# Last attention's rope scores as two fp32r products over 128 rows, another order of ScalarE's copies and exps, two-product gate projections, a 352-wide input projection

## The reference

```python
# block 1: the forget gate is a projection of 16 columns of w_in
log_f = log_sigmoid(f_logit + b_forget); cum = cumsum(log_f)
...
# layer A: u = rms_norm(x) @ w_in; 8 of its columns are the gates
gates = gates + b_if
i_pre, log_f = gates[..., :4], log_sigmoid(gates[..., 4:])
...
# layer C
u = rms_norm(x, norm_g) @ w_in
cq, ckv, kpe, z = split(u, [384, 384 + 256, 384 + 256 + 64])
q = (rms_norm(cq, q_norm_g) @ w_uq).reshape(B, S, 8, 192)
kv = (rms_norm(ckv, kv_norm_g) @ w_ukv).reshape(B, S, 8, 128 + 128)
k = concatenate([k_nope, broadcast(kpe)])            # 128 + 64 columns a head
q = rms_norm(q, qn_g); k = rms_norm(k, kn_g)
q, k = [nope, rope(last 64 columns, cos, sin)]
s = einsum('bhqd,bhkd->bhqk', q, k) * 192 ** -0.5     # blocks of the causal mask: 128 x 128
o = softmax(s) @ v * silu(z);  x + o @ w_out
```

## Time and profile before

| | |
|---|---|
| median of the runs | 1853.67 us |
| lowest, highest | 1852.9, 1855.1 us |
| profiled execution, its time | 1853.72 us |
| its span in the profile | 1851.6 us |
| PE busy | 1729.0 us, 93% |
| DVE busy | 1157.1 us, 62% |
| ACT busy | 987.3 us, 53% |
| POOL busy | 230.9 us, 12% |

### The profile page before, as it was taken

One profiled execution on the slowest core, in us unless ns is written; L12 is line 12 of the kernel. 1 busy time (PEld: TensorE's weight loads), 2 busy tenths in 40 slices (PEclk: granted clock), 3 DMA queues, 4 the chain that ended last, 5 costly groups with the idle time before them and its releaser, 6 DMA issues.

```text
span 1851.6 us, 23252 instructions
## 1 busy us (share of the span) xinstructions
PE 1729.0 (93%) x8654; PEld 1411.6 (76%) x8654; DVE 1157.1 (62%) x1652; ACT 987.3 (53%) x1368; POOL 230.9 (12%) x172
## 2 busy tenths in 40 slices
PE   6999999999999599999999994899999999999899
PEld 5888888888888577777777773788788878888567
DVE  3543435445564699999999997761647643437562
ACT  4222335444433489999888995554353223548540
POOL 0000001010000124444233331010010000000000
PEclk9999999999999699999999997899999999999999
DMA  6755357435144699999999995232023332222001
GB/s 143 103 104 83 111 92 64 67 60 65 46 148 185 228 399 422 420 422 421 421 423 420 422 419 208 80 114 91 23 82 101 114 115 91 86 71 94 24 1 69
DMA packets 127043, 326.47 MB, mean 176 GB/s; under 512 B 8176, under 2 KB 80624, under 8 KB 118768
## 3 DMA queue, kind: packets, MB, share of 16 engines
q1 hardware_dynamic: 121360, 315.85, 52.0%
q0 software_dynamic: 5168, 8.92, 1.3%
q10 hardware_dynamic: 432, 0.56, 0.1%
HBM read 319.02 MB, written 15.21 MB: 181 GB/s over the span
## 4 chain that ended last, share of the span: by engine, by line
PE 69%; DMA 10%; DVE 9%; issue 7%; ACT 4%; DVEq 0%; SPq 0%; ACTq 0%; POOLq 0%; POOL 0%
PE bank L1455 14%; PE bank L1457 14%; PE bank L1456 14%; DMA down<-in_w_e_down 6%; PE turned L1455 4%; PE turned L1456 4%; PE turned L1457 4%; PE bank L1791 2%; DMA gate<-in_w_e_gate 2%; DVE down_lo L2379 2%; PE bank L1535 2%; PE bank L1631 2%; DVE gate_lo L2379 2%; DVE up_lo L2379 1%; PE bank L2007 1%
## 5 line engine op out<-in xcount | busy, mean ns | idle before, releaser
L2041 DVE TENSOR_TENSOR w_lo<-w_raw,w_hi 128x2048 fp32r<-128x2048 f32 (+2 forms) x76 | 163.7, 2157 | 290.4 <-ACT w_hi L903 286.5
L903 ACT ACTIVATE w_hi<-w_raw 128x2048 fp32r<-128x2048 f32 (+3 forms) x132 | 169.3, 1306 | 279.1 <-DMA w_raw<-in_w_in 74.8
L1455 PE MATMUL bank<-h1T_hi,w_hi 128*128 128x512 f32 x376 | 151.1, 402 | 0.0
L1457 PE MATMUL bank<-h1T_hi,w_lo 128*128 128x512 f32 x376 | 147.4, 392 | 0.0
L1456 PE MATMUL bank<-h1T_lo,w_hi 128*128 128x512 f32 x376 | 146.7, 390 | 0.0
L2379 DVE TENSOR_TENSOR down_lo<-down,down_hi 128x2048 fp32r<-128x2048 f32 x62 | 139.0, 2281 | 3.4 <-ACT down_hi L903 3.3
L2379 DVE TENSOR_TENSOR gate_lo<-gate,gate_hi 128x2048 fp32r<-128x2048 f32 x64 | 128.8, 2016 | 0.0
L2379 DVE TENSOR_TENSOR up_lo<-up,up_hi 128x2048 fp32r<-128x2048 f32 x64 | 126.5, 2016 | 0.2 <-ACT up_hi L903 0.2
L903 ACT ACTIVATE down_hi<-down 128x2048 fp32r<-128x2048 f32 x62 | 115.1, 1905 | 17.8 <-DMA down<-in_w_e_down 17.7
L824 POOL COPY put_row<-table 64x1 int32 (+1 forms) x31 | 82.8, 2671 | 257.2 <-DVE ys L2414 257.2
L903 ACT ACTIVATE gate_hi<-gate 128x2048 fp32r<-128x2048 f32 x64 | 108.7, 1700 | 10.6 <-DMA gate<-in_w_e_gate 10.6
(11 more groups left out here) (679 smaller groups left out, 4451.5 us busy)
## 6 DMA issues: line engine op xcount, KB each, us to landing
gate<-in_w_e_gate SPq DMA_DIRECT2D x32, 2048.0 KB, 17.3
up<-in_w_e_up SPq DMA_DIRECT2D x32, 2048.0 KB, 17.7
down<-in_w_e_down SPq DMA_DIRECT2D x31, 2048.0 KB
w_raw<-in_w_in SPq DMA_DIRECT2D x24, 1024.0 KB, 9.2
...
```

The lines of the kernel that those rows point to most:

```text
L903: return nc.scalar.activation(out, in_, ACT.Copy, scale=scale)
L1455: pe.matmul(out, sh, mh, start=start, stop=False)
L1457: return pe.matmul(out, sl, mh, start=False, stop=stop)
L2041: V.tensor_tensor(ring_view(w_lo, n), ring_view(raw, n), ring_view(w_hi, n).bitcast(F32), ALU.subtract)\
```

## The change

1. ACT gets a tiny Sqrt at the start, behind its DMAs and a memset on DVE, ahead of the squares.
2. `narrow`: DVE writes the low part of the weights into the upper 64 columns of w_hi, half as many elements. PE multiplies this pair with the high and the low part of the activations, 8 x 2 products. Rows 64 to 127 of the bank then hold the products of the low weights; DVE adds both halves, in `log_gate` and for g_i.
3. The 704 columns of the input are cut in 352 + 352, both in two slices of 4 chunks.
4. The 64-row product of the rope scores becomes two of 128 rows in fp32r. The moving operand rope_k holds the high part of k twice (own rows and the other 64), the other operand rope_q the high and the low part of q; the second product takes the low part of k in rope_k_lo, also twice. ACT makes rope_k (`rope_keys`), POOL the other two, in four operations a head, one head ahead, in two sets of buffers that are free when the head two before has its last scores. PE waits for POOL's `rope_split` at each head's first item. p and nb move to other buffers.
5. In ACT's attention loop `among(step)` comes first, then the pT copy of item step - 3, then the exp of item step - 1. The key work and the splits of out3 move by one or two steps, on ACT and DVE.

```diff
+CIN = (QL + KVL + ROPE) // 2
...
-LAST_KEYS = 9
+LAST_KEYS = 10
...
-        p3_t = [temp(f"p3_t{b}", b) for b in (1, 2, 0, 4)]
+        p3_t = [big(f"p3_t{b}", 2, shape=(P, SEQ), extra=2048 * b) for b in range(4)]
+        rope_q, rope_k, rope_k_lo = ([temp(f"{name}0", n, dt=F32R), big(f"{name}1", 3, F32R, (P, SEQ), 2048 * m)]
+                                     for m, (name, n) in enumerate((("rope_q", 0), ("rope_k", 1), ("rope_k_lo", 11))))
...
-        nb3 = temp("nb3", 11, (P, 8))
+        nb3 = temp("nb3", 7, (P, 8), extra=1024)
...
-        add_wide("cin", 0, cols_of(t["c_w_in"], 0, 512), KC, 512)
-        add_slice(("cin", 1, 0), cols_of(t["c_w_in"], 512, 192), KC, 192)
+        for n in range(2):
+            add_wide("cin", n, cols_of(t["c_w_in"], CIN * n, CIN), KC, CIN)
...
+        narrow_slices = (slice_no[("forget", 0)], slice_no[("gates", 0)])
...
+            for h in range(CH):
+                p, own, other = h % 2, half_rows(h % 2), half_rows(1 - h % 2)
+                if h >= 2:
+                    pool.wait_ge(results, order[("S3", TT * (h - 2) + TT - 1)] + 1)
+                elif h == 1:
+                    pool.wait_ge(results, order[("ukv", 3, TT - 1)] + 1)
+                else:
+                    pool.wait_ge(sem("q_roped"), 1)
+                until_taken(pool, ("qpT", h // 2))
+                step(nc.gpsimd.tensor_copy(rope_q[p][own, :], qpT[own, h // 2, :]))
+                nc.gpsimd.tensor_tensor(rope_q[p][other, :], qpT[own, h // 2, :], rope_q[p][own, :].bitcast(F32), ALU.subtract)
+                pool.wait_ge(sem("rope_k_made"), h + 1)
+                step(nc.gpsimd.tensor_tensor(rope_k_lo[p][own, :], kpT[own, h // 2, :], rope_k[p][own, :].bitcast(F32), ALU.subtract))
+                nc.gpsimd.tensor_copy(rope_k_lo[p][other, :], rope_k_lo[p][own, :]).then_inc(sem("rope_split"), 1)
...
+            act.wait_ge(sem("mark_set"), 1)
+            step(nc.scalar.activation(mark[:, 3:4], mark[:, 5:6], ACT.Sqrt))
             for tt in range(TT):
                 act.wait_ge(x_loaded[tt], 16)
...
-                for i in range(n_items + LAG):
-                    k = i - LAG
+                for step_ in range(n_items + LAG):
+                    among(step_)
+                    k, i = step_ - LAG, step_ - 1
                     if k >= 0 and k % 2 == 0:
                         keys = (k % TT + 1) * P
                         src = until_made(act, (PT, k))
                         if k >= 2:
                             act.wait_ge(results, order[(O, k - 2)] + 1)
                         took(copy(pT_buf[k % 2][:, 0:k % TT + 1, :], src[:, 0:keys].rearrange("p (k q) -> p k q", q=P)), (PT, k))
-                    if i < n_items:
+                    if 0 <= i < n_items:
...
-                        among(i)
...
-            for s, n in enumerate((512, 192)):
-                if s == 0:
-                    split_wide("cin", 0, KC, n_slices)
-                else:
-                    split(slice_no[("cin", 1, 0)] + 2, n_slices)
+            for s in range(2):
+                split_wide("cin", s, KC, n_slices)
                 for tt in range(TT):
                     src = until_made(act, ("cin", s, tt))
-                    took(copy(c_tok[:, tt, 512 * s:512 * s + n], src[:, 0:n], r_fin[:, tt:tt + 1]), ("cin", s, tt))
+                    took(copy(c_tok[:, tt, CIN * s:CIN * s + CIN], src[:, 0:CIN], r_fin[:, tt:tt + 1]), ("cin", s, tt))
...
+            def rope_keys(h):
+                until_taken(act, ("kpT", h // 2))
+                if h >= 2:
+                    act.wait_ge(results, order[("S3", TT * (h - 2) + TT - 1)] + 1)
+                else:
+                    act.wait_ge(sem("q_roped"), 1)
+                for x in (h % 2, 1 - h % 2):
+                    ins = copy(rope_k[h % 2][half_rows(x), :], kpT[half_rows(h % 2), h // 2, :])
+                ins.then_inc(sem("rope_k_made"), 1)
             def among3(i):
-                if i == 1:
+                if i % TT == 0 and i // TT + 1 < CH:
+                    rope_keys(i // TT + 1)
+                if i == 2:
                     key_squares(3)
-                elif i == 3:
+                elif i == 4:
                     take_root(16)
                 elif i == LAST_KEYS:
                     evict_k(3)
-                elif i in (3 * TT, 4 * TT):
+                elif i in (3 * TT + 2, 4 * TT + 2):
                     split(slice_no[("out3", 0, i // TT - 3)], n_slices)
...
+                if s == 2:
+                    rope_keys(0)
...
-                wh, wl = weights(slice_no[key])
+                w_both, _ = weights(slice_no[key])
                 out = open_bank(pe, key)
                 for c in range(KC):
-                    ins = parts3(out[:, :], wh[:, c, :], wl[:, c, :], xh[:, c, :], xl[:, c, :], c == 0, c == KC - 1)
+                    pe.matmul(out[:, :], w_both[:, c, :], xh[:, c, :], start=c == 0, stop=False)
+                    ins = pe.matmul(out[:, :], w_both[:, c, :], xl[:, c, :], start=False, stop=c == KC - 1)
                 ins.then_inc(results, 1)
...
-            token_wide("cin", 0, 512, h3_terms, tile_ready=lambda b, tt: until_taken(pe, ("x4T", b, tt)),
+            token_wide("cin", 0, CIN, h3_terms, tile_ready=lambda b, tt: until_taken(pe, ("x4T", b, tt)),
                        between={(0, 0): lambda: turn_x4(1, TT - 1)})
-            wh, wl = weights(slice_no[("cin", 1, 0)])
-            for tt in range(TT):
-                out = open_bank(pe, ("cin", 1, tt))
-                tk = slice(tt * P, (tt + 1) * P)
-                for c in range(KC):
-                    ins = parts3(out[:, 0:192], hT_hi[2][:, c, tk], hT_lo[2][:, c, tk], wh[:, c, :], wl[:, c, :], c == 0, c == KC - 1)
-                ins.then_inc(results, 1)
+            token_wide("cin", 1, CIN, h3_terms)
...
             def scores3(i, out):
                 h, qt = i // TT, i % TT
-                rows, c, n = slice(64 * (h % 2), 64 * (h % 2) + 64), h // 2, (qt + 1) * P
+                p, n = h % 2, (qt + 1) * P
+                if qt == 0:
+                    pe.wait_ge(sem("rope_split"), h + 1)
                 pe.matmul(out[:, 0:n], qnT[:, h, qt * P:n], knT[:, h, 0:n], start=True, stop=False)
-                pe.matmul(out[:, 0:n], qpT[rows, c, qt * P:n], kpT[rows, c, 0:n], start=False, stop=False)
+                pe.matmul(out[:, 0:n], rope_q[p][:, qt * P:n], rope_k[p][:, 0:n], start=False, stop=False)
+                pe.matmul(out[:, 0:n], rope_q[p][:, qt * P:n], rope_k_lo[p][:, 0:n], start=False, stop=False)
                 return pe.matmul(out[:, qt * P:n], id_b[:, :], block_b[:, :], start=False, stop=True)
...
-                if first_gained <= n < end_gained:
+                if n in narrow_slices:
+                    V.tensor_tensor(ring_view(w_hi, n)[:, :, P // 2:], ring_view(raw, n)[:, :, 0:P // 2],
+                                    ring_view(w_hi, n)[:, :, 0:P // 2].bitcast(F32), ALU.subtract).then_inc(w_lo_made, 1)
+                elif first_gained <= n < end_gained:
...
+            V.memset(mark[:, 5:6], 1.0).then_inc(sem("mark_set"), 1)
...
-            def log_gate(src, x, ab, logs, one, bias, made, log_made):
-                step(V.tensor_scalar(x[:, :], src, bias, None, ALU.add))
+            def log_gate(src, low, x, ab, logs, one, bias, made, log_made):
+                step(V.tensor_copy(x[:, :], low))
+                step(V.scalar_tensor_tensor(out=x[:, :], in0=src, scalar=bias, in1=x[:, :], op0=ALU.add, op1=ALU.add))
...
-            step(V.tensor_scalar(g_i[:, :], src[0:MH, :], vec[0:MH, V_BI:V_BI + 1], None, ALU.add))
-            log_gate(src[LO:LO + MH, :], g_x, g_abs, g_l, g_one, vec[0:MH, V_BG:V_BG + 1], sem("g_abs_made"), sem("g_log_made"))
+            step(V.tensor_copy(g_i[:, :], src[P // 2:P // 2 + MH, :]))
+            step(V.scalar_tensor_tensor(out=g_i[:, :], in0=src[0:MH, :], scalar=vec[0:MH, V_BI:V_BI + 1], in1=g_i[:, :],
+                                        op0=ALU.add, op1=ALU.add))
+            log_gate(src[LO:LO + MH, :], src[P // 2 + LO:P // 2 + LO + MH, :], g_x, g_abs, g_l, g_one, vec[0:MH, V_BG:V_BG + 1], sem("g_abs_made"), sem("g_log_made"))
...
-            split_wide("cin", 0, KC, n_slices)
-            until_made(dve, ("cin", 0, TT - 1))
-            split(slice_no[("cin", 1, 0)] + 2, n_slices)
+            for n in range(2):
+                split_wide("cin", n, KC, n_slices)
+                until_made(dve, ("cin", n, TT - 1))
...
-                elif i == 5:
+                elif i == 6:
                     key_rows(3)
-                elif i == 6:
+                elif i == 8:
                     key_ropes(3)
-                elif i in (3 * TT, 4 * TT):
+                elif i in (3 * TT + 2, 4 * TT + 2):
                     split(slice_no[("out3", 0, i // TT - 3)], n_slices)
```

2 lines of the change are left out of this document (1 added, 1 removed).

## The result

The changed kernel took 1842.94 us, median of four runs (1839.87 to 1845.23), beside 1853.85 for the kernel before (four runs, 1852.9 to 1855.1): a ratio of 0.9936, 95% interval 0.9924 to 0.9948, 10.9 us less. Forecast were 1840.4, 13.3 us less, with a range of 1835.4 to 1845.6.

A forecast was written before the change was run, and what follows sets the result against it. TensorE, busy for 93% of the span, was taken as the bound. 1.28 + 0.42 + 0.6 + 2.0 + 10.6 + 2.4 - 4.0 = 13.3 us off 1853.7 gave 1840.4 us, range 1835.4 to 1845.6.

The forecast's parts named there:

- Term 1: Start of the kernel: Sqrt table load issued ahead of ACT's squares, so root comes earlier; gain 1.28 us.
- half-kept bound: Start of the kernel, lower bound: if the clock rises at a fixed moment, only half, 0.6 us, is kept.
- Term 2: Narrow gates: fewer products, partly eaten by new waits; gain 0.42 us at forget, 0.6 us at layer A's gates.
- Term 3: 704-column input: 192 products of 352 columns replace 96 of 512 and 96 of 192; gain 2.0 us.
- Term 4: Last attention's rope scores: two 128-row products replace one of 64 rows; gain 1.32 us a head, 10.6 in eight.
- Term 5: Waits in the last attention: ACT's new order leaves 5.3 of 7.7 us; gain 2.4 us, bounds 0 and 7.
- Term 6: Last attention: POOL's new rope operations hold up DVE's nb, so PE waits for the pT copy; loss 4.0 us.
- No collision: Rival, last attention: nb gets in before POOL or is too short to matter; 1836.4 us, chance 26%.
- ScalarE becomes the pace: Rival, last attention: ACT's rope copies at head boundaries are exposed, up to 8.4 us lost; 1844.6 to 1848.8, chance 14%.
- POOL becomes the pace: Rival, last attention: POOL's four operations take more than a head, 7.9 us; 1855.0 us, slower, chance 4%.
- The doubled table switch: Rival, start: removed table switch worth twice its row, PE's first product 2.6 us earlier; 1839.1 us, chance 4%.
- The exclusion as a rule: Last attention: read strictly, POOL first in all six heads, loss 6.0 us, the sum 2.0 us worse.

The follow-up runs named there:

- again: The changed kernel itself, unchanged, run and profiled a second time: 1842.7 us, ratio 0.993.
- before_look: The kernel before, unchanged, one execution for a second profile of it: 1855.03 us.
- start_only: The kernel before with only the start's memset and small Sqrt added: 1853.97 us, ratio 1.0002.
- order_only: The changed kernel without its rope scores: old 64-row product, no rope copies on ACT, no POOL loop; 1843.91 us, ratio 0.9938.
- nb_scalar: The changed kernel with DVE making nb as tensor times per-row scalar instead of a product of two tensors: 1840.65 us, ratio 0.9927.
- rope_early: The changed kernel with head 0's rope work on ACT and POOL moved, head 1's ACT rope copies behind the first exp: 1838.55 us, ratio 0.9907.
- final: The changed kernel with nb by scalar, moved rope work, half splits of out3, later last keys, early exp table, om split ahead: 1835.89 us, ratio 0.9897.
- both: The changed kernel with nb by a per-row scalar and the moved rope work of heads 0 and 1 together: 1838.34 us, ratio 0.9915.
- no_pool: The changed kernel with POOL's rope work for heads 0 and 1 only, for its time alone: 1839.67 us, ratio 0.9925.
- rope_only: The changed kernel with ACT's old attention loop, old places of key work and splits, rope copies behind each head's first exp: 1861.06 us, ratio 1.0038.
- exp_first: The changed kernel with ACT's exp put back ahead of the pT copy, nothing else: 1846.22 us, ratio 0.9948.

## Why the prediction was right, and where it was not

The time lies inside the range, 2.5 us over the forecast, and the sign and size of the gain were right. The terms were not, and that the sum came out is in good part luck: in the attention the products and the order brought 16.6 + 8.2 = 24.8 us where 13.0 was forecast, and new waits took 12.1 of it back (24.8 - 12.7, again), where 4.0 was; 2.5 more went ahead of it and the start's 1.7 did not arrive.

- **Term 1, the start, 1.28.** The mechanism was right to 0.1 us: root 1.16 earlier, PE's first product 1.15 against 1.28. The sentence that what is gained before the experts passes through them was wrong: in both profiles of the changed kernel nothing of it is left behind them. The half-kept bound did not go low enough. Three causes are seen. The first products run slow for a time that varies; the first dense product came at 23.93 and 24.55 in two profiles of before, and at 22.5 to 25.7 in the twelve with the early Sqrt. Near 319 us ACT waits for a weight, and longer than before, ACT before and after:

```profile
319.23 0.63 ACT L903 ACTIVATE w_hi<-w_raw 128x512 fp32r<-128x512 f32 x1 [1.80 <-DMA w_raw<-in_w_in]
```
```profile
319.12 0.63 ACT L922 ACTIVATE w_hi<-w_raw 128x512 fp32r<-128x512 f32 x1 [3.34 <-DMA w_raw<-in_w_in]
```

  ACT had come there 1.65 us earlier and is 0.11 earlier behind it. The windows of 300 to 322 us have a DMA share of 1.00 before and after. But it is not that the weight lands at a fixed time: this wait was 1.7 to 1.9 us in before, before_look, start_only, order_only and nb_scalar, though ACT came 0.4 to 0.5 us earlier in the last three, and 3.0 to 3.3 us in all others, in rope_early too, where ACT came 0.4 us later than before. What decides between the two is not shown. Third, 1.6 to 1.7 us went at 512 to 516 us, where the granted clock was 0.60 after, 0.57 again, 1.00 before and in start_only; seven of the eleven profiles with both early changes have this drop. Drops of the same kind stand in the expert stage of every kernel, one in before (892 us) and after (894), two in before_look (925, 955) and again (860, 925), and each moves what follows by 1.6 to 1.7 us, so that a gain of 1.3 us can't be read from one profile there. The last 0.5 to 0.8 us of after's and again's loss was not settled.
- **Term 2, gates, 0.42 + 0.6.** Forget: the new wait was 1.34 against 1.4, and the stage gained 0.3; lost again with the start's. Gates: a wait of 1.25 against 1.2, copies of 0.69 against 0.7, gain 0.47 against 0.6. final shows the other side: with the split ahead of the chain the wait is gone.
- **Term 3, the input, 2.0.** 33.09 - 31.06 = 2.03. With the gates' 0.47 that is 2.5 us for the stage from the experts to c_tok, and 1.7 to 2.2 arrived there. Of the difference 0.2 us each is lost at two products in layer A that begin a new part, at 1361.42 and 1408.93 after, and in the profiles of the variants too; why was not traced.
- **Term 4, the rope products, 10.6.** The direction was right and the size too small: 2.08 us a head, 16.6 in all. The pair of the first attention in the earlier trace rows was read with what runs out of the product ahead of it. Beside the 128-row product that this attention has anyway, the pair adds 1.33 - 0.96 = 0.37 us for 512 columns, not 0.55 (0.96 is from 1774.41 to 1775.37). A head without long waits took 9.16 us before and takes 7.42, not "about 7.9": 2.08 less for the products, 0.33 more for the new small wait.
- **Term 5, the order, 2.4 with bounds of 0 and 7.** It was the step that failed most: order_only has 7.4 of the 8.2 us of waits gone and 8.2 us less. I kept 3.6 us for the first heads and 0.85 twice for splits because I treated these waits as the amount of work on ACT and DVE. They were its sequence. The same work in another order leaves 0.8 us of waits, in the last head, as long as PE's scores are slow.
- **Term 6, the collision, -4.0.** The mechanism, its place and even the tie were right: PE waits of 1.26 us against 1.3, 0.47 in the two heads with splits against 0.4. But not in six heads: at 1736.23 and 1772.60 nb was not held, and in the first, at 1726.26, PE's wait was 0.53. By way of nb it cost about 2 us in three heads (1.06 of the wait of 1.26 and 0.47 of each of two, nb_scalar), of which 0.9 to 1.4 came back when nb was freed (nb_scalar beside after, both beside rope_early). Missing was every other DVE operation of two tensors: kr twice ahead of the attention and once in it. I had looked for the collision only in the loop that the change speaks of, while POOL's head 0 starts 44 us ahead of it. With the clock's drop that cost 2.5 to 4.1 us, and 1.1 in the attention.
- **What new waits there were besides.** The splits: 1.1 to 1.2 us each, where I had 0.85 each; a head of PE is shorter now than I had it. The first exp: 2.0 us, because rope_keys(1) and a table load stand ahead of it; this I had left inside the 5.3.

**The rivals.** "No collision" (26%) is refuted by nb's and kr's rows, by nb_scalar and by no_pool, though nb's own price was 2 us and not 4. "ScalarE becomes the pace" (14%) did not happen, because of the other order, and happens at once without it: rope_only, 1861. I had priced it at 8.4 us with the new order in place, and not asked what the order is there for. "POOL becomes the pace" is out: its four operations took 3.95 to 4.35 us a head from the third on, 4.35 beside DVE's splits, and no PE wait names it. The doubled table switch is out, with root 1.16 us earlier and not 2.6.

**The exclusion as a rule.** The Trainium skill (SBUF — State Buffer, "Who interferes with whom") has DVE instructions with two SBUF inputs and GpSimd ones that read SBUF exclude each other; by that rule I had 2.0 us more of loss. The rows agree with the rule in kind, from both sides: nb with a scalar is free, and POOL's cast at 1754.09 took 1.00 us in place of 0.61 while DVE's split ran until 1754.62. What did not hold was my strict reading, POOL first in all six heads. Nor is it enough that POOL's row starts first: where the two start together, nb's row is 0 to 5 ns behind POOL's in the twelve cases in which it was not held and 6 to 9 ns behind in the seven in which it was (starts to the nanosecond in the traces of after, again, rope_early, exp_first, rope_only).
